# A chunked triangular inversion stored without its zero blocks: products of 64 by 64 in place of 128 by 128

## The reference, cut to what matters

```
def step(S, inp):
    r_t, w_t, k_t, v_t, kk_t, a_t = inp
    s_kk = jnp.einsum('bhvk,bhk->bhv', S, kk_t)
    S = (S * w_t[:, :, None, :] - s_kk[..., None] * (kk_t * a_t)[:, :, None, :]
         + v_t[..., :, None] * k_t[:, :, None, :])
    return S, jnp.einsum('bhvk,bhk->bhv', S, r_t)
```

## Time and profile before

| | us |
|---|---|
| median of 3 runs | 1755.24 |
| the profiled execution | 1755.07 |
| its span | 1753.3 |
| TensorE matmul records busy in the span | 1693.3 |
| VectorE busy | 875.3 |
| ScalarE busy | 674.9 |
| GpSimd busy | 129.9 |

### The profile page before, as it was taken

How to read it: one execution, slowest core, us unless ns; L and a number is a source line. 1 busy time by engine, 2 the same in 40 slices (tenths; PEclk the granted TensorE clock), 3 DMA queues, 4 the chain that set the end, 5 groups by cost and what they waited for, 6 DMA issues and landing times.

```text
span 1753.3 us, 22293 instructions
## 1 busy us (share of the span) xinstructions
PE 1693.3 (97%) x8770; PEld 1377.0 (79%) x8770; DVE 875.3 (50%) x1169; ACT 674.9 (38%) x1017; POOL 129.9 (7%) x126
## 2 busy tenths in 40 slices
PE   7999999999999999999999999998998899999997
PEld 6777778878777778888888778877986778888886
DVE  5633445642444665444333685776446454444333
ACT  5145564215565333333223544364132333333221
POOL 0001002000100200000001300001320200000000
PEclk9999999999999999999999999989999999999998
DMA  5312212331222222233333321210011232223331
GB/s 190 131 61 85 73 61 84 108 120 61 85 73 67 78 85 96 97 97 94 99 99 108 106 73 61 67 37 1 1 31 50 71 108 97 96 96 91 96 95 56
DMA packets 40745, 143.92 MB, mean 82 GB/s; under 512 B 4816, under 2 KB 4832, under 8 KB 40384
## 3 DMA queue, kind: packets, MB, share of 16 engines
q1 hardware_dynamic: 37008, 130.87, 23.4%
q0 software_dynamic: 2192, 8.73, 1.6%
q10 hardware_dynamic: 1440, 2.88, 0.5%
HBM read 140.37 MB, written 2.10 MB: 81 GB/s over the span
## 4 chain that ended last, share of the span: by engine, by line
PE 81%; DVE 12%; ACT 5%; issue 1%; DMA 0%; POOL 0%; DVEq 0%; ACTq 0%; SPq 0%
PE bank L451 23%; PE bank L452 22%; PE bank L453 22%; PE bank L433 6%; DVE sb_w_low L1147 2%; PE bank L439 2%; ACT sb_w_high L1891 1%; PE bank L669 1%; PE bank L648 1%; PE bank L605 1%; DVE sb_xg_low L1155 1%; DVE sb_E L1147 1%; PE bank L793 1%; DVE sb_x L1147 1%; DVE sb_rot L1147 1%
## 5 line engine op out<-in xcount | busy, mean ns | idle before, releaser
L1147 DVE TENSOR_TENSOR sb_w_low<-sb_raw,sb_w_high 128x1024 fp32r<-128x1024 f32 (+1 forms) x253 | 311.1, 1230 | 389.3 <-ACT sb_w_high L1891 383.3
L451 PE MATMUL bank<-sb_xg_high,sb_w_high 128*128 128x512 f32 x1176 | 469.1, 399 | 23.8 <-DVE sb_xg_low L1155 15.4
L453 PE MATMUL bank<-sb_xg_high,sb_w_low 128*128 128x512 f32 x1176 | 461.8, 393 | 0.0
L452 PE MATMUL bank<-sb_xg_low,sb_w_high 128*128 128x512 f32 x1176 | 461.7, 393 | 0.0
L1891 ACT ACTIVATE sb_w_high<-sb_raw 128x1024 fp32r<-128x1024 f32 (+1 forms) x253 | 263.2, 1040 | 355.1 <-PE bank L453 324.6
L451 PEld LDWEIGHTS bank<-sb_xg_high,sb_w_high 128*128 128x128 f32 x1176 | 222.7, 189 | 89.9 <-issue 31.9
L453 PEld LDWEIGHTS bank<-sb_xg_high,sb_w_low 128*128 128x128 f32 x1176 | 223.0, 190 | 47.8
L452 PEld LDWEIGHTS bank<-sb_xg_low,sb_w_high 128*128 128x128 f32 x1176 | 223.1, 190 | 44.6
L453 PE MATMUL bank<-sb_h_high,sb_w_low 128*128 128x512 f32 x352 | 137.0, 389 | 0.0
L452 PE MATMUL bank<-sb_h_low,sb_w_high 128*128 128x512 f32 x352 | 137.0, 389 | 0.0
L451 PE MATMUL bank<-sb_h_high,sb_w_high 128*128 128x512 f32 x352 | 137.0, 389 | 0.0
(11 more groups left out here) (338 smaller groups left out, 2063.8 us busy)
## 6 DMA issues: line engine op xcount, KB each, us to landing
sb_raw<-w_ffn_in SPq DMA_DIRECT2D x88, 512.0 KB, 3.4
sb_raw<-w_ffn_out SPq DMA_DIRECT2D x32, 512.0 KB, 3.5
sb_raw<-w_tok SPq DMA_DIRECT2D x24, 512.0 KB, 3.8
sb_raw<-w_mix_f SPq DMA_DIRECT2D x18, 512.0 KB, 3.3
sb_raw<-w_rot SPq DMA_DIRECT2D x16, 512.0 KB, 3.6
sb_raw<-w_qk SPq DMA_DIRECT2D x16, 512.0 KB, 3.3
sb_raw<-w_out SPq DMA_DIRECT2D x16, 512.0 KB, 3.3
sb_raw<-w_ffn_out SPq DMA_DIRECT2D x16, 384.0 KB, 3.1
```

The lines of the kernel that those rows point to most:

```text
L451: e.matmul(out, w[0], v[0], start=first, stop=False)
L452: e.matmul(out, w[0], v[1], start=False, stop=False)
L453: return e.matmul(out, w[1], v[0], start=False, stop=last)
L1147: e.tensor_tensor(out, a, b, op).then_inc(*v.up(*signal))
```

## The change

The matrices X, XT, AT, CT, Pm, A_ak, M_rk and M_rb keep only the diagonal blocks: the first chunk of a tile lies in partitions 0 to 63 and the second in 64 to 127, and a tile takes 64 columns in place of 128. Each matrix of a head is 128 by 256 in place of 128 by 512. Every product of a tile becomes two products with weights of 64 by 64, one in the rows and columns 0 to 63 of the array and one in 64 to 127. Both write to the same bank, in their half of the partitions. The steps' compact results are 32 columns a tile. `gram` makes for each tile, chunk and head one product of 64 by 64. `W2T` is made for a head pair at once, with a bank for each chunk. A group now signals once, with its last product. The masks shrink to 64 columns, with two new tables, and the loaded table of constants grows from 1920 to 2176 columns.

```
-        def per_tile(key, freed_by, left, right, out):
+        def per_chunk(key, freed_by, left, right, out):
             i = take(key, freed_by)
             for t in range(TT):
-                group(out(banks[i], t), [(left(t), right(t))], *key)
+                for c in (0, 1):
+                    made = e.matmul(out(banks[i], t, c), left(t, c), right(t, c), start=True, stop=True)
+            made.then_inc(*p.up(*key))
...
-                for h, i in zip(two, out):
-                    r, f = head_tile(h)
-                    made = e.matmul(banks[i][:, blk(t)], left[r, f, blk(t)], right[r, f, blk(t)], start=True, stop=True)
+                for c in (0, 1):
+                    for h, i in zip(two, out):
+                        r, f = head_tile(h)
+                        at = slice(P * t + CHUNK * c, P * t + CHUNK * c + CHUNK)
+                        made = e.matmul(banks[i][rows_of(c), in_chunk(t)], left[r, f, at], right[r, f, at],
+                                        start=True, stop=True)
...
-            compact = lambda b, t, size=size: b[:, t * 64:(t + 1) * 64].rearrange("p (n c) -> p n c", c=size)
+            compact = lambda b, t, c, size=size: b[rows_of(c), t * 32:(t + 1) * 32].rearrange("p (n c) -> p n c", c=size)
...
+            out = [take(("W2T product", f, c), ("W2T", 2 * f + c)) for c in (0, 1)]
+            for t in range(TT):
+                for h in two:
+                    for c in (0, 1):
+                        made = e.matmul(banks[out[c]][head_tile(h)[0], in_chunk(t)],
+                                        m.tokA[rows_of(c), t, h * 64:(h + 1) * 64], m.XT[rows_of(c), h, in_chunk(t)],
+                                        start=True, stop=True)
...
-                    e.matmul(banks[o][:, o_cols], m.M_rk[:, h, blk(t)], m.tokB[:, t, v_cols], start=False,
-                             stop=False, skip_group_check=True)
+                    for half in (0, 1):
+                        q = rows_of(half)
+                        e.matmul(banks[o][q, o_cols], m.M_rk[q, h, in_chunk(t)], m.tokB[q, t, v_cols], start=False,
+                                 stop=False, skip_group_check=True)
...
-            tt(tiles(out), tiles(bank(what, h)[:, :]), over_tiles(mask), ALU.mult, what, h)
+            tt(chunks(out), chunks(bank(what, h)[:, 0:TT * CHUNK]), over_tiles(mask), ALU.mult, what, h)
...
-                tt(part, part, bank(what + " step", size, h)[:, 0:256].rearrange("p (n c) -> p n c", c=size),
+                tt(part, part, bank(what + " step", size, h)[:, 0:128].rearrange("p (n c) -> p n c", c=size),
...
-                act(tiles(out[:, h, :]), over_tiles(mem.ident), name + " preset")
+                act(chunks(out[:, h, :]), over_tiles(mem.table("chunk_ident")), name + " preset")
...
-                act(m.Pm[:, h, :], bank("Pm product", size, h)[:, :], "Pm", size, h)
+                act(m.Pm[:, h, :], bank("Pm product", size, h)[:, 0:TT * CHUNK], "Pm", size, h)
...
-            tt(tiles(m.CT[:, h % 2, :]), tiles(m.AT[:, h, :]), over_tiles(mem.pairs(size)), ALU.mult,
+            tt(chunks(m.CT[:, h % 2, :]), chunks(m.AT[:, h, :]), over_tiles(mem.chunk_pairs(size)), ALU.mult,
```

More of the change, by code:

```diff
@@ L70 @@
 N_SHARED = 128
-MIXER = {"same_head": (0, 128), "before": (128, 128), "upto": (256, 128), "pairs": (384, 7 * 128),
-         "pairs_ts": (384 + 896, 128), "restart": (1408, 512)}
-N_MIXER = 1920
+MIXER = {"same_head": (0, 128), "before": (128, 64), "upto": (192, 64), "pairs": (256, 7 * 128),
+         "pairs_ts": (1152, 64), "restart": (1216, 512), "chunk_pairs": (1728, 6 * 64), "chunk_ident": (2112, 64)}
+N_MIXER = 2176
 SHARED_BY = {}
@@ L342, in pairs, with chunk_pairs @@
         return self.table("pairs")[:, n * P:(n + 1) * P]
+    def chunk_pairs(self, m):
+        n = LEVELS.index(m) - 1
+        return self.table("chunk_pairs")[:, n * CHUNK:(n + 1) * CHUNK]
     def pair_mask(self, m, n_tiles):
@@ L986, in side_products @@
                     p.wait_ge(*of("tokB", TT - 1))
-                    per_tile(("Gv product", h), ("Gv", h), tile_of(m.A_ak[:, h % 2, :]),
-                             lambda t: m_tokB(t, v_cols), cols64)
+                    per_chunk(("Gv product", h), ("Gv", h), chunk_of(m.A_ak[:, h % 2, :]),
+                              lambda t, c: m.tokB[rows_of(c), t, v_cols], whole)
                     yield
@@ L1003, in product @@
                 p.wait_ge(*of("X made", size, h))
-                per_tile(("Pm product", size, h), ("Pm", size, h), tile_of(m.CT[:, h % 2, :]), tile_of(m.X[:, h, :]),
-                         whole)
+                per_chunk(("Pm product", size, h), ("Pm", size, h), chunk_of(m.CT[:, h % 2, :]),
+                          chunk_of(m.X[:, h, :]), whole)
             def updates(h):
@@ L1010, in updates @@
                 if size < 32:
[L1011 to L1014, removed]
+                    per_chunk(("X step", size, h), ("X made", 2 * size, h), chunk_of(m.XT[:, h, :]),
+                              half_of(m.Pm[:, h, :], False), compact)
+                per_chunk(("XT step", size, h), ("XT made", 2 * size, h), chunk_of(m.Pm[:, h, :]),
+                          half_of(m.XT[:, h, :], True), compact)
             product(0)
@@ L1027, in inverse @@
             pass
[L1028 to L1035, removed]
+        for two in HEAD_PAIRS:
+            for h in two:
+                p.wait_ge(*of("Gv", h))
+                p.wait_ge(*of("XT made", 64, h))
+                per_chunk(("W1 product", h), ("W1", h), chunk_of(m.XT[:, h, :]), chunk_of(m.Gv[:, h, :]), whole)
+            f = two[0] // 2
+            out = [take(("W2T product", f, c), ("W2T", 2 * f + c)) for c in (0, 1)]
+            for t in range(TT):
+                for h in two:
+                    for c in (0, 1):
+                        made = e.matmul(banks[out[c]][head_tile(h)[0], in_chunk(t)],
+                                        m.tokA[rows_of(c), t, h * 64:(h + 1) * 64], m.XT[rows_of(c), h, in_chunk(t)],
+                                        start=True, stop=True)
+                        if t == TT - 1 and h % 2:
+                            made.then_inc(*p.up("W2T product", f, c))
     def recurrence(m):
@@ L1732, in first_pairs @@
             v.wait_ge(*v.before())
-            e.copy_predicated(tiles(ap), over_tiles(mask).bitcast(I32), tiles(bank(what, h)[:, :])).then_inc(*v.up(*signal))
+            e.copy_predicated(chunks(ap), over_tiles(mask).bitcast(I32),
+                              chunks(bank(what, h)[:, 0:TT * CHUNK])).then_inc(*v.up(*signal))
         v.wait_ge(*of("X preset"))
@@ L1776, in inverse @@
             pass
[L1777 to L1780, removed]
+        for f in range(2):
+            for c in (0, 1):
+                v.wait_ge(*of("W2T product", f, c))
+                ts(m.W2T[:, :, f, rows_of(c)], chunks(bank("W2T product", f, c)[:, 0:TT * CHUNK]), 1.0, None,
+                   ALU.mult, ALU.bypass, "W2T", 2 * f + c)
     def recurrence(m):
```

45 lines of the change are left out of this document (27 added, 18 removed).

## The result

The kernel after takes 1730.99 us (median of 4 runs, 1727.45 to 1731.77) where the kernel before took 1755.24 beside it (median of 4, 1753.74 to 1767.87): a ratio of 0.9841, 95% interval 0.9806 to 0.9876. The forecast was 1727.4, the range 1719 to 1741. The profiled execution took 1731.77 us with a span of 1729.9, so the span fell by 23.4 us.

A forecast was written before the change was run, and what follows sets the result against it. TensorE, paced by weight loads, was taken to bound the doubling loop. Start -2.3, loop -25.2, tail -0.5, recurrence -0.9 and new idle +1.2 gave -27.7, so 1727.4 us; stated range 1719 to 1741, the forecast's own 1721 to 1734.

The forecast's parts named there:

- The bound and the pace: Doubling loop: TensorE bounds it, weight loads set the pace; a 64 by 64 product takes 0.058 us, 0.029 a record.
- The lower bound's 0.107: Product time in the array: half of 0.107 if both load and stream halve, giving 0.053 us a product.
- Rival B: Groups writing both halves to one bank: the halves exclude each other, a group stays at 0.90 us; 1752 us, chance 0.05.
- Rival C: TensorE records: a cost per record, such as 0.056 us, eats every saving through the doubled count; 1759 us, chance 0.08.
- Rival A: Loop's instruction supply: 9 packet fetches leave up to 1.2 us open each, 11 us back; 1738 us, chance 0.10.
- The grams: Gram products, six in the loop: each becomes 32 records in 0.93 us instead of 16 in 1.09.
- the loop's saving: Doubling loop up to the last Pm product: 34.3 us against 59.5, 25.2 us saved.
- The wait for Pm: Loop, after the Pm products of heads 0 and 1: TensorE waits 0.25 us a level, 1.0 in four levels.
- The start: VectorE's operations and ScalarE's Pm copy ahead of the loop halve their columns; first step starts 2.3 us earlier.
- The tail: Loop's end to the fence: GpSimd's untouched 10.3 us on offset and gate set the end; only 0.5 us saved.
- The idle ahead of the recurrence: TensorE idles 4.6 us before the first state; the lower clock behind it costs 1.2 us, between 0 and 2.
- The later tiles: Recurrence blocks after the first: the wait for y_rwkv grows by what is saved; 0.9 us counted overall, 3.5 as bound.

The follow-up runs named there:

- micro: Kernel after, three groups of unread 64 by 64 products (one, two, four quadrants) replacing five unread products ahead of the inversion: 0.059, 0.031, 0.015 us a record.
- tile_busy: Kernel after, with two unread products ahead of the transposes ending each of the recurrence's first three tiles: 1727.72 us, ratio 0.9824 to the kernel before.
- c_order: Kernel after, a group's two loops exchanged: four products of the first chunk, then four of the second. Median 1742.19 us, ratio 0.9909 to the kernel before.

## Why the prediction was right, point by point

**The bound and the pace: right.** TensorE set the stage, and the product of 64 by 64 came at the forecast 0.058 us, two records of 0.029, in opposite quadrants and one bank. `micro` shows the reason given, halves beside each other, by itself. (The lower bound's 0.107 stands in none of its rows; half of the 0.105 from the earlier trace rows gives the same 0.053.)

**Rival B: false**, by the loop's trace: one bank, 0.029 us a record. The rule of the Trainium skill, TensorEngine Tiling (Array Packing), "Gotcha 1: PSUM Pressure", on which it stood, does not show here for opposite quadrants: one bank in the loop goes at 0.029, two banks in `micro` at 0.031. The trace agrees with what the prediction took from the Trainium skill, PSUM — Partial Sum Buffer, "PSUM bank collisions raise a hardware error". **Rival C: false**: a record can start every 0.015 us. **Rival A: nearly nothing**: the loop fetched 9 packets of instructions, as worked out, and all gaps of PE in the loop add up to 0.7 us.

**The grams: mis-sized.** The forecast took 0.93 us for 32 records; they take 0.5 to 0.57, since two heads and two chunks fill all four quadrants. Six of them in the loop are worth 2 to 2.5 us. That would have made the loop's saving some 27.6; it is 25.9, mostly since 6.1 us of it were at 1.2 GHz and not 3.4, worth 1.4 more. That these two nearly cancel is luck. The wait for Pm, 0.25 a level in the forecast, is there: the Pm products of heads 0 and 1 hold the step behind them to 1.12 us for 32 records (1227.07 to 1228.19) where their own pace gives 0.94; it is too short to show as idle, since a record lasts 0.27.

**The start: the term of 2.3 us was 1.2.** The operations shrank to the forecast 0.42 and 0.45 us, but the sum of 2.85 for them left out the wait of 0.46 ahead of the last copy, which stayed; so up to the square it was 1.7 us less and not 2.15. The square then took 0.5 more, held by GpSimd's CT. Because the smaller masked copies ended sooner, GpSimd's operation now started first. The transposes ahead of it ran at 1.2 GHz (0.43 us apart from 1207.2), which made AT of head 2 later by 0.2.

**The tail: right.** GpSimd's chain became the last ahead of the fence and TensorE idled 5.0 us (forecast 4.6).

**The idle ahead of the recurrence: right.** The stretch at 1.2 GHz behind it makes the first M block (lines 1093 and 1095 before, 1122 and 1126 after) start 1.2 us later behind the fence, 13.9 us in place of 12.7: "1.2 us, between 0 and 2". The block itself gives back 0.7, not 0.9 (1.81 to 1.07 us). Together +0.4 to +0.5 against +0.3.

**The later tiles: the step that failed.** "there the wait grows by what is saved": so it did, 0.89 to 1.75 us at the first such place, and up to that point nothing more is won or lost. But the prediction put the clock behind these waits at nothing, and so its +0.3 for the whole part came out at +3.6, where its bounds reach +1.1 (2 less 0.9). Behind the first two of these waits the clock fell for 3.4 us each: from the first transposes to the second +1.6, from there to the third +1.5, and nothing from there to the end. `tile_busy` shows the price by taking it away, and `c_order` shows it by not paying it. Whether it is paid differs between executions, so part of the +3.1 is the luck of the two profiles.

Against the forecast's sum of -27.7 the profiled span fell by 4.3 less: 0.6 ahead of the change, 1.1 at the start and 3.3 here, less 0.7 that the loop gave more.

## What to carry to other kernels

A saving on the bounding engine that a later wait absorbs isn't always free: behind waits of 0.97 to 5 us TensorE went to 1.2 GHz for 3.4 or 6.8 us in some executions and not in others, so each such wait behind the change is a term of the sum with a range (0 to 1.6 us each at y_rwkv), and unread products of the wait's length take it back. Where work is taken off TensorE by half, look for the chain on a slow engine that it covered, and place that chain in gaps where the fast engine reads from PSUM; moving the wait alone only turns it into contention. Products of 64 by 64 pay only where several quadrants are at work; with four of them the pace was 0.015 us a record.

## What the runs showed of the hardware

- Paces add up over quadrants: 0.059, 0.031 and 0.015 us a record in one, two and four (float32, 64 by 64, 64 columns), and the overlap doesn't need alternation: runs of 8 records to one quadrant overlap with the next group's run in the other, at 0.52 to 0.57 us a group in place of 0.44 to 0.49.
- The clock can stay down: in the profiled `c_order` it fell in a wait of 2.6 us and stayed at 1.2 GHz for 64 us, in which TensorE was never idle; by their times and mean clocks four of its eight runs were of this kind (20 us each). With alternating quadrants it came back after 6.8 us. Why the order makes that difference wasn't tested.
- The same kernel doesn't always fall at the same wait: behind 1.75 and 2.53 us it fell in the kernel after and not in `c_order`; a fall of 3.4 us cost 1.5 or 1.6.
- VectorE and GpSimd hold each other for whole operations: 1.22 became 1.71, 1.27 became 2.29, and 1.4 became 5.1 us for two.
